# Condition vectors against two weight chunks at a time in a two-block transformer kernel

## The reference, cut to what matters

```python
    cond = jax.nn.silu(c)
    ...
        mod = cond @ w_ada[l] + b_ada[l]
        sh1, sc1, g1, sh2, sc2, g2 = jnp.split(mod[:, None, :], 6, axis=-1)

        h = rms_norm(x, norm1_w[l]) * (1 + sc1) + sh1
        proj = h @ w_in[l]
    ...
def ada_mod(cond, w, b):
    m = jax.nn.silu(cond) @ w + b
    return jnp.split(m[..., None, :], 6, axis=-1)
```

## Time and profile before

| what | us |
|---|---|
| median of 3 runs | 1687.81 |
| lowest and highest of them | 1685.01, 1690.80 |
| the profiled execution, its own time | 1684.95 |
| its span, from first to last instruction | 1683.1 |
| PE busy in the span | 1341.7 |
| DVE busy | 624.9 |
| ACT busy | 294.8 |

### The profile page before, as it was taken

The page is one execution under the profiler, slowest core; times in us unless marked ns, Lnnn a source line. Parts: engine busy times, 40 slices in busy tenths (PEclk is TensorE's granted clock), DMA queues, the critical chain, the costliest instruction groups (busy, mean ns, idle before and its releaser), DMA issues.

```text
span 1683.1 us, 23534 instructions
## 1 busy us (share of the span) xinstructions
PE 1341.7 (80%) x10014; PEld 828.1 (49%) x10015; DVE 624.9 (37%) x1116; ACT 294.8 (18%) x565; POOL 5.0 (0%) x10
## 2 busy tenths in 40 slices
PE   6898998577766756675776666567999999999997
PEld 4797763124212212221221222123768999989997
DVE  2666452061100101010010101004667878775555
ACT  2015420010000000000000000001344343443433
POOL 1000000000000000000000000000000000000000
PEclk8999999889888878877887888789999999999999
DMA  9989979999999999999999999998306887635451
GB/s 399 368 331 421 428 293 398 431 431 429 430 432 432 430 431 432 432 430 431 431 432 431 430 432 432 431 430 360 151 1 259 337 334 292 262 139 199 176 200 50
DMA packets 48567, 589.95 MB, mean 351 GB/s; under 512 B 5708, under 2 KB 8172, under 8 KB 9848
## 3 DMA queue, kind: packets, MB, share of 16 engines
q1 hardware_dynamic: 44912, 583.72, 83.0%
q10 hardware_dynamic: 3592, 5.31, 0.9%
HBM read 586.39 MB, written 2.62 MB: 350 GB/s over the span
## 4 chain that ended last, share of the span: by engine, by line
DMA 51%; PE 40%; DVE 6%; ACT 2%; issue 1%; SPq 0%; DVEq 0%; ACTq 0%
DMA ring<-in_w 47%; PE ps L2198 5%; PE ps L2193 5%; PE ps L2194 5%; PE ps L1679 3%; PE ps L1989 3%; PE ps L2010 3%; PE ps L1870 2%; PE ps L2207 2%; PE ps L2209 2%; PE ps L2208 2%; DMA ring<-in_w_in 2%; DMA ring<-in_w_ada 2%; PE ps L1609 1%; PE ps L2147 1%
## 5 line engine op out<-in xcount | busy, mean ns | idle before, releaser
L1989 PE MATMUL ps<-ring,mixT 128*32 128x512 f32 x2016 | 299.6, 731 | 169.4 <-DMA ring<-in_w 164.1
L2010 PE MATMUL ps<-ring,arena 128*32 128x512 f32 x1024 | 169.2, 796 | 105.0 <-DMA ring<-in_w 91.6
L1989 PEld LDWEIGHTS ps<-ring,mixT 128*32 128x32 f32 x2016 | 61.9, 122 | 379.8 <-DMA ring<-in_w 188.9
L886 DVE TENSOR_TENSOR ring_parts<-ring,ring_parts 128x1024 fp32r<-128x1024 f32 (+3 forms) x119 | 189.6, 1625 | 77.9 <-ACT ring_parts L821 77.5
L1274 DVE TENSOR_TENSOR arena<-arena,ps 128x512 f32<-128x512 f32 x16 | 11.0, 688 | 491.6 <-PE ps L1989 491.6
L2193 PE MATMUL ps<-mixT_parts,ring_parts 128*128 128x256 f32 x704 | 169.5, 281 | 0.6 <-issue 0.3
L2194 PE MATMUL ps<-mixT_parts,ring_parts 128*128 128x256 f32 x704 | 169.3, 281 | 0.0
L821 ACT ACTIVATE ring_parts<-ring 128x1024 fp32r<-128x1024 f32 x126 | 124.1, 1050 | 158.2 <-DMA ring<-in_f 158.2
L2010 PEld LDWEIGHTS ps<-ring,arena 128*32 128x32 f32 x1024 | 32.5, 128 | 223.5 <-DMA ring<-in_w 143.0
L706 ACT ACTIVATE arena<-ps 128x512 f32<-128x512 f32 x16 | 9.6, 597 | 756.6 <-PE ps L1989 756.6
L2193 PEld LDWEIGHTS ps<-mixT_parts,ring_parts 128*128 128x128 f32 x704 | 133.2, 189 | 2.1 <-issue 0.7
(11 more groups left out here) (416 smaller groups left out, 1433.3 us busy)
## 6 DMA issues: line engine op xcount, KB each, us to landing
ring<-in_w SPq DMA_DIRECT2D x190, 2048.0 KB, 25.8
ring<-in_f SPq DMA_DIRECT2D x22, 2048.0 KB, 8.0
ring<-in_w_ada SPq DMA_DIRECT2D x12, 2048.0 KB, 15.2
ring<-in_ada_w SPq DMA_DIRECT2D x12, 2048.0 KB, 15.7
ring<-in_f SPq DMA_DIRECT2D x22, 1024.0 KB, 7.4
modrow<-in_adaT SPq DMA_DIRECT2D x12, 1024.0 KB, 9.0
arena<-in_adaT SPq DMA_DIRECT2D x12, 1024.0 KB, 9.9
ring<-in_w_in SPq DMA_DIRECT2D x5, 2048.0 KB, 18.2
```

Source lines behind the costliest of these rows:

```text
L886: return tt(out.bitcast(F32R), v, hi, ALU.subtract)
L1989: last = mm(ps[rows[u], j, :], XeT[:, 2 * m + k, rows[u]], w[:, u, k * FE:(k + 1) * FE], start=(m == 0 and k == 0), stop=(m == 3 and k == 1))
L2010: last = mm(ps[rows[u], m, :], heT[:, k, rows[u]], w[:, u, m * 512:(m + 1) * 512], start=(k == 0), stop=(k == FE // P - 1))
```

## The change

`ada_chunk` is replaced by `ada_pair`, which takes two chunks in neighbouring slots. It waits for both, and each matmul takes 128 columns of the one and 128 of the other as its moving operand, 256 in all; the results lie beside each other in the accumulator, where the two chunks had theirs before. A pair is 32 matmuls where two chunks were 64, for the same number of columns. `ring_used` rises by two at the pair's end, where it rose by one after each chunk. The first pairs are (0, 1) and (2, 3). In the attention the 12 chunks become six pairs, and the table of their places changes with it.

```diff
-            def ada_chunk(n, bank, s, cset, i=None, signal=True):
-
-                arrived(n, i)
-                w = ring_view(n, KD)
+            def ada_pair(n, bank, s, cset):
+
+                assert n % NS < NS - 1 and s % 4 < 3
+                arrived(n)
+                arrived(n + 1)
+                w = ring[:, n % NS:n % NS + 2, :]
                 for k in range(KD):
                     for j in range(4):
-                        last = mm(ps[32 * j:32 * j + 32, bank + s // 4, (s % 4) * P:(s % 4 + 1) * P], cond[:, cset, k, :],
-                                  w[:, k, j * P:(j + 1) * P], start=(k == 0), stop=(k == KD - 1))
-                if signal:
-                    last.then_inc(ring_used, 1)
+                        last = mm(ps[32 * j:32 * j + 32, bank + s // 4, (s % 4) * P:(s % 4 + 2) * P], cond[:, cset, k, :],
+                                  w[:, :, k * 512 + j * P:k * 512 + (j + 1) * P], start=(k == 0), stop=(k == KD - 1))
+                last.then_inc(ring_used, 2)
...
-            for c in range(4):
-                ada_chunk(RA[c], 0, c, 0)
+            for c in (0, 2):
+                ada_pair(RA[c], 0, c, 0)
...
             def ada(n):
-                if n == 6:
+                if n == 3:
                     pe.wait_ge(ada_ev, 4)
-                ada_chunk(RL0 + n, 0, n % NS, 1)
-
-            ada_chunk(RA[10], 6, 2, 0)
-            ada_chunk(RA[11], 6, 3, 0)
+                ada_pair(RL0 + 2 * n, 0, 2 * n % NS, 1)
+
+            ada_pair(RA[10], 6, 2, 0)
...
-            for u, (a, b, c) in enumerate((((1, 2), (), (3,)), ((4, 5), (6,), ()), ((7, 8), (9,), ()), ((10, 11), (), ()))):
+            for u, (a, b, c) in enumerate((((1,), (), ()), ((2,), (3,), ()), ((4,), (), ()), ((5,), (), ()))):
```

More of the change, by code:

```diff
@@ L1716, in _ @@
             tokens(RW[1], 512, 256, [ps[:, 3, t * 256:(t + 1) * 256] for t in range(NT)], None).then_inc(ring_used, 2)
-            ada_chunk(RA[4], 6, 0, 0)
-            ada_chunk(RA[5], 6, 1, 0)
+            ada_pair(RA[4], 6, 0, 0)
             features(RW[3], 512, 4, 0, low_parts(1, 2)).then_inc(ring_used, 2)
@@ L1735, in _ @@
             last.then_inc(hidT_tr, 1)
-            ada_chunk(RA[6], 6, 2, 0)
-            ada_chunk(RA[7], 6, 3, 0)
+            ada_pair(RA[6], 6, 2, 0)
             pe.wait_ge(hidT_ev, 1)
@@ L1752, in _ @@
             pe.wait_ge(ada_ev, 2)
-            ada_chunk(RA[8], 6, 0, 0)
-            ada_chunk(RA[9], 6, 1, 0)
+            ada_pair(RA[8], 6, 0, 0)
             pe.wait_ge(win_dve, 1)
```

## The result

The change makes the kernel slower. The median of 7 runs is 1694.58 us (1691.72 to 1697.17), beside 1688.02 us (1683.93 to 1690.80, 7 runs) of the kernel before; the ratio is 1.0044, 95% interval 1.0033 to 1.0055. The same program run again beside other kernels gave 1.0034 (1.0022 to 1.0046). The forecast was 1688.5 with a range up to 1694.0 and 0.84 on "same"; the measured time lies above the range, and the change, 6.6 us between the medians, is clear of the noise. The profiled execution took 1693.87 us with a span of 1692.0, which is 8.9 us more span than the profiled execution before; that one lay low among its runs, so the two profiles show more than the medians do.

What follows compares the result with a forecast made beforehand. Bound: the expert-weight DMA stream, whose start hangs on PE's chain. Terms 1684.95 + 1.7 - 0.3 + 0 + 0 = 1686.4 us for the profiled execution; on the mean, 1687.14 + 1.4 = 1688.5 us, range 1683.5 to 1694.0.

Steps and rivals of the forecast that it cites:

- The bound: Expert-weight DMA stream from 260 us: starts as much later as PE reaches the output projection later; everything behind shifts whole.
- The product: Matmuls of 256 columns instead of 128: save 0.04 us a pair, eight pairs on PE's chain, -0.3 us.
- The divided operand: Rival: each product's jump between slots costs PE 27 ns, 13.8 us over eight pairs, 1702 us; chance 0.05.
- The late slots: First chunk's slot freed 1.8 us later, touching loads 12 and 20: cost 0; as rival +3.6 us, chance 0.07.
- The wait for chunks 2 and 3: Front: chunk 2 now runs behind chunk 3's landing, pair takes 5.1 us partly at low clock, +1.7 us.
- Its upper end of 6.8 us: Pair (2, 3) in the front wholly at the low clock takes 6.8 us, +3.4 us.
- The attention: First attention from 145 us, pairs in new places: ends where it did, 0, between -1.4 and +0.5 us.
- the rival's +1.5 us: Attention between 155.6 and 161.4 us: if the clock falls, a 3.0 us stretch runs at half rate, +1.5 us.
- The low clock: Rival: pair (2, 3) wholly at low clock and clock falling in the attention, +4.6 us, 1691.7 us; chance 0.12.

Runs made afterwards that it cites:

- x_pairs: Kernel before with only the pairs (6, 7), (14, 15), (18, 19) and (24, 25) joined; 1686.01 us, ratio 1.0000.
- x_no67: Changed kernel with chunks 6 and 7 one by one, so load 12 is asked for when chunk 6 is done; ratio 1.0034.
- x_att: Kernel before with pairs only in the attention, in their new places, front as before; 1688.88 us, ratio 1.0009.
- x_no23: Changed kernel with chunks 2 and 3 one by one as they land; 1690.30 us, ratio 1.0017.
- x_wait: Kernel before with one wait more: chunk 2 not started before chunk 3 has landed, chunks single; 1690.80 us, ratio 1.0023.
- x_best: Changed kernel with chunks 2 and 3 one by one and unused matmuls filling PE's waits in front and attention; 1682.43 us, ratio 0.9974.
- x_beforefill: Kernel before with unused matmuls filling PE's waits in the front and the attention; 1684.91 us, ratio 0.9995.
- x_front: Changed kernel with pairs in the front only, the attention's 12 chunks single in their old places; 1688.72 us, ratio 1.0007.
- x_places: Kernel before with its 12 single attention chunks moved to the places the pairs have after the change; 1689.19 us, ratio 1.0020.

## Why the prediction was wrong, point by point

**The bound was right.** The stream starts as much later as the projection does. From the first product of the projection to the stream's end it was 957.9 us before and 958.4 after, and from there to the end of the span 523.8 both times. In all 14 profiles the first of these lies between 956.7 and 959.4 us. The chain of argument from PE's front to the end of the program held.

**The product was right.** Every pair at the whole clock took 3.66 us, and `x_pairs` came out at 1.0000. The divided operand costs nothing that shows.

**The late slots were right.** `x_no67` gives the slot back earlier and gains nothing.

**The wait for chunks 2 and 3 was mis-sized.** The mechanism was named, +1.7 us. It measured 5.62 - 3.39 = 2.2 us in the profile after. In the six profiles with that wait and no fills in the front, the read-out stands at 40.6 to 41.7 us, in the five without it and without fills at 37.8 to 38.7: 2.8 us apart in the mean. Two things were wrong in the term. The 3.0 us from PE's restart to the rise of the clock, read off one row, became 4.0 in this profile and 5.5 in the second one, where the pair took 6.33 us. And chunk 3 alone was taken at 3.39 us, where `x_att` and `x_no23` show 2.79 and 2.74: in these two the clock had risen during chunk 2, stood at the whole as chunk 3 began and fell within it. In `x_att`:

```profile
32.00:33.00 1.00, 0.93 (x24) 0.62 (x16) 0.00 (x0) 0.00 (x0) 0.00 (x0) 0.75 0.73 309
34.97 2.79 PE L1609 MATMUL ps<-ring,cond 128*32 128x128 f32 x64 [2.04 <-DMA ring<-in_w_ada]
35.00:36.00 1.00, 1.00 (x36) 1.00 (x40) 0.00 (x0) 0.00 (x0) 0.00 (x0) 0.96 1.22 503
36.00:37.00 1.00, 1.00 (x28) 0.99 (x23) 0.00 (x0) 0.00 (x0) 0.00 (x0) 0.50 0.82 337
```

Across the profiles without fills the work behind the landing took 5.62 to 6.33 us with the wait and 2.74 to 3.54 without it, so the term lay anywhere between 2.1 and 3.6. Its upper end of 6.8 us for the pair was low as well: chunk 3's 3.39 us had a part at the whole clock, and twice chunk 2's 3.64, all of it at the low one, is 7.3.

Behind the read-out the front lost more. The same two groups of profiles stand 3.5 us apart at the split of load 12 and 3.7 at `queries(0)` (144.7 and 141.1), so most of the further 0.9 us is there by the time load 12 is split. From load 10's issue to that split it takes 20.4 to 21.7 us in the six with the wait and 19.4 to 20.6 in the five without it, 1.2 apart in the mean. The slots do not explain that, by `x_no67`. What stands beside it are the small loads that ACT issues between 55.8 and 60.7 us in these kernels, hardly later or earlier with the wait. With the wait they are issued ahead of load 10 or just beside it and nearly all have landed within some 3 us; without it they come behind load 10, and `wr`, the largest of them, landed 17.7 us or more after its issue. Microseconds to landing in before, `x_no23` and `x_wait`:

```profile
wr<-in_wr ACTq DMA_DIRECT2D x1, 288.0 KB, 25.3
wr<-in_wr ACTq DMA_DIRECT2D x1, 288.0 KB, 18.1
wr<-in_wr ACTq DMA_DIRECT2D x1, 288.0 KB, 3.5
```

So a front that is 2 us late lets these loads in ahead of loads 10 to 12. That this costs the 1.2 us is argued from the traces; no run moved ACT's loads.

**The attention is the step that failed.** It was costed at 0, and measured +4.1 us in the profile. Its parts went as worked out: no idle ahead of `scores(1)`, `scores(2)` on DVE's copy 1.4 us earlier relative to the front's shift (I had 1.2), and the transposes of step 2 uncovered for 1.42 us by ACT's L646. What was wrong was the sentence that set the low clock aside: that PE had gone on at the whole clock after 1.47 us of idle. The same trace had a case that spoke the other way and was not looked at, the low stretch from 150 us on behind 1.85 us of idle. And in the profile before, the chunk of 1.95 us stood right behind the 1.47 us. The change took it away, and the pair ahead of it ended earlier, so that PE was busy for only 2.2 of the 6.1 us up to `scores(2)`, with 1.84, 1.48 and 0.58 us of idle in them. The clock fell as `scores(2)` began, and stayed down for 6.8 us, not for the 3.0 of the earlier trace rows; the rival's +1.5 us was a third of the 4.1 to 4.75 us that it measured. The one profile is no accident here: the attention takes 60.1 to 60.7 us in the four profiles with the old order and 64.0 to 65.3 in the six with the new one. As I had moved work into one idle time, I counted the idle time filled as free, and did not count the idle times that were opened as a price, since nothing on the chain waited for them.

**The chances.** The low clock was among the rivals with 0.12 and at 1691.7 us. It is what happened in the attention, at about three times its price there; in the front the pair did not run at the low clock throughout, as that rival had it, but for 4.0 of its 5.62 us. The result lies 2.9 us above the rival. Putting the measured differences in place of the terms, 3.7 for the front and 4.1 for the attention, with what the pairs save already in them, gives +7.8; the medians say +6.6 and +6.4. The difference is not settled; the profile before lay low among its runs.

## What to carry to other kernels

Where small matmuls fill an engine's waits, they have a second use beside their own work, to keep the clock up; before moving them, look at how thin the work becomes in the places that they leave, and not only at the chain. Joining two pieces of work that arrive at different times costs the first one's work behind the second one's arrival, and costs it at the low clock if the wait grows. A longer operand does not repay that when the products were already bound by their columns.

## What the runs showed of the hardware

- The moving operand may come from two places 16 KB apart in each partition: 64 records of 256 columns, four products side by side, took 3.66 us, in one piece or in two.
- The low clock did not end a fixed time after the work began. In six profiled executions with the wait and nothing between, the clock rose 4.0 to 5.5 us after PE took up work behind chunk 3's landing, and that work took 5.62, 5.63, 5.66, 5.74, 5.75 and 6.33 us. In three with PE idle for 1.8 us ahead of chunk 3 it rose after 3.0 to 3.3 us.
- Of the 14 profiles, 13 show low stretches of the clock between 20 and 260 us, the other two with filled gaps in the front among them; only `x_best` shows none, and it was the fastest of all.
- Within the records of a single chunk PE sometimes stands idle for 0.35 to 0.57 us, put down to issue: four times in the attentions of `x_beforefill`, `x_front` and `x_places`, all with 128-column products. What it waits for there was not tried.
